# A hybrid attention and state-space layer: five places of local kernels on SyncE and three on ScalarE, feature stores held for two weight blocks, and the rest of u loaded in three parts

## The reference, cut to what matters

```python
h = rmsnorm(x, norm_mix_pre)
z = h @ w_in
q, k, v, u, gates = jnp.split(z, splits, axis=-1)
y_attn = windowed_gqa_sink(q, k, v, attn_sink) @ w_branch_attn
y_ssm = s5_bidirectional(u, ...) @ w_branch_ssm
g = jax.nn.sigmoid(gates.reshape(bsz, seq, N_BRANCH, D_MODEL))
merged = g[:, :, 0] * y_attn + g[:, :, 1] * y_ssm
x = x + rmsnorm(merged @ w_out, norm_mix_post)
# then a feed-forward block: gelu(dwconv3(h2 W_gate)) * (h2 W_up), W_down, rmsnorm
```

## Time and profile before

| | us |
|---|---|
| time before, median of 3 (2640.09 to 2646.72) | 2644.09 |
| the profiled execution's own time | 2639.97 |
| its span | 2638.2 |
| TensorE busy in the span | 2532.5 |
| input projection, to TensorE's first attention matmul | 0 to 264.3 |
| attention, to the first matmul on u | to 463.2 |
| gates and states, to TensorE's last matmul on the states | to 896.9 |

### The profile page before, as it was taken

One profiled execution on the slowest core, in us unless ns is written; L12 is line 12 of the kernel. 1 busy time (PEld: TensorE's weight loads), 2 busy tenths in 40 slices (PEclk: granted clock), 3 DMA queues, 4 the chain that ended last, 5 costly groups with the idle time before them and its releaser, 6 DMA issues. The chain is left out here.

```text
span 2638.2 us, 34575 instructions
## 1 busy us (share of the span) xinstructions
PE 2532.5 (96%) x12222; PEld 2082.1 (79%) x12222; DVE 1655.7 (63%) x2255; ACT 968.8 (37%) x1754; POOL 1022.0 (39%) x1217
## 2 busy tenths in 40 slices
PE   7999898999999899999989999999999999999898
PEld 6877786788887688888868888877888887788786
DVE  5201765795970184544687767788766776675876
ACT  5221776512212350124453333343333334532432
POOL 2073564387830000012244354335344435443543
PEclk9999999999999899999999999999999999999999
DMA  6483878644446636464424222224222224455465
GB/s 215 137 273 111 179 179 232 212 144 148 156 172 163 176 127 236 175 164 151 153 88 151 74 90 86 72 66 132 87 90 81 79 75 144 166 196 203 152 208 183
DMA packets 317957, 390.98 MB, mean 148 GB/s; under 512 B 51936, under 2 KB 250080, under 8 KB 309472
## 3 DMA queue, kind: packets, MB, share of 16 engines
q1 hardware_dynamic: 270816, 309.66, 38.0%
q10 hardware_dynamic: 41184, 46.78, 5.3%
q0 software_dynamic: 5792, 32.38, 3.4%
HBM read 255.07 MB, written 133.69 MB: 147 GB/s over the span
## 5 line engine op out<-in xcount | busy, mean ns | idle before, releaser
L531 PE MATMUL tl_banks<-gu_b_hi,gu_a_hi 128*128 128x512 f32 x1848 | 727.3, 394 | 32.0 <-DVE gu_b_lo L1988 18.5
L533 PE MATMUL tl_banks<-gu_b_lo,gu_a_hi 128*128 128x512 f32 x1848 | 724.4, 392 | 0.0
L532 PE MATMUL tl_banks<-gu_b_hi,gu_a_lo 128*128 128x512 f32 x1848 | 723.9, 392 | 0.0
L531 PEld LDWEIGHTS tl_banks<-gu_b_hi,gu_a_hi 128*128 128x128 f32 x1848 | 350.0, 189 | 116.8 <-issue 31.5
L533 PEld LDWEIGHTS tl_banks<-gu_b_lo,gu_a_hi 128*128 128x128 f32 x1848 | 349.5, 189 | 73.1
L532 PEld LDWEIGHTS tl_banks<-gu_b_hi,gu_a_lo 128*128 128x128 f32 x1848 | 350.1, 189 | 71.9
L1982 DVE TENSOR_TENSOR gu_a_lo<-gu_raw,gu_a_hi 128x512 fp32r<-128x512 f32 (+1 forms) x340 | 296.8, 874 | 148.2 <-ACT gu_a_hi L1679 148.1
L1679 ACT ACTIVATE gu_a_hi<-gu_raw 128x512 fp32r<-128x512 f32 (+1 forms) x340 | 208.7, 616 | 347.1 <-PE tl_banks L533 297.5
L1354 POOL TENSOR_TENSOR gu_s_one<-gu_raw 128x512 f32<-128x512 f32 (+1 forms) x68 | 91.7, 1349 | 344.3 <-DVE gu_a_lo L1982 206.6
L1367 POOL TENSOR_TENSOR gu_raw<-gu_s_one,gu_raw 128x512 f32<-128x512 f32 (+1 forms) x68 | 97.8, 1439 | 166.7 <-DVE gu_a_lo L1982 166.3
L148 PE MATMUL pi_banks<-pi_feat_hi,pi_w_hi 128*128 128x512 f32 (+1 forms) x344 | 132.2, 384 | 10.1 <-DVE pi_feat_lo L333 6.1
(11 more groups left out here) (315 smaller groups left out, 5001.1 us busy)
## 6 DMA issues: line engine op xcount, KB each, us to landing
gu_raw<-in_w_ffn_gate SPq DMA_DIRECT2D x44, 512.0 KB, 3.6
gu_raw<-in_w_ffn_up SPq DMA_DIRECT2D x44, 512.0 KB, 3.5
gs_w_raw<-in_w_in SPq DMA_DIRECT2D x40, 512.0 KB, 4.4
br_rows<-gates POOLq DMA_DIRECT2D x16, 1024.0 KB, 7.2
gu_raw<-f SPq DMA_DIRECT2D x32, 512.0 KB, 3.9
dn_y<-down_sums SPq DMA_DIRECT2D x16, 1024.0 KB, 4.9
down_sums<-dn_y SPq DMA_DIRECT2D x15, 1024.0 KB, 5.9
f<-gu_conv SPq DMA_DIRECT2D x11, 1025.0 KB, 5.1
```

The lines of the kernel that those rows point to most:

```text
L531: pe.matmul(out, w_hi, x_hi, start=first, stop=False, skip_group_check=again)
L532: pe.matmul(out, w_lo, x_hi, start=False, stop=False, skip_group_check=again)
L533: return pe.matmul(out, w_hi, x_lo, start=False, stop=last, skip_group_check=again)
```

## The change

The change has three parts. In the input projection SyncE waits for the last product of block 5 before it stores feature chunk 2, and for the last product of block 6 before chunk 3. At the end of attention SyncE issues five of the eight places of the local kernels and ScalarE, after its last copy, the other three; GpSimd issues none. In the last part of gates and states, u's rest comes in three parts (groups 17 to 20, 10 to 16, 0 to 9); partitions 0 to 63 still come by SyncE, partitions 64 to 127 by GpSimd, which waits for the last gate product; ScalarE loads none. Each half of a part has a semaphore of its own.

```diff
@@ stage_project_in, sync
             store_features(1)
             load_weights(8)
+            sync.wait_ge(product_done, number[5, CHUNKS - 1] + 1)
             store_features(2)
             load_weights(9)
+            sync.wait_ge(product_done, number[6, CHUNKS - 1] + 1)
             store_features(3)
@@ attention_and_tables
+    BY_SYNC = 5
         sync.wait_ge(kernels_ready, 1)
-        for l in range(SSM_L // 2):
+        for l in range(BY_SYNC):
             place_local(sync, l, local_placed)
@@ gpsimd
-        pool.wait_ge(kernels_ready, 1)
-        for l in range(SSM_L // 2, SSM_L):
-            place_local(pool, l, local_late)
@@ scalar
         copy_share(TILES - 1)
+        act.wait_ge(kernels_ready, 1)
+        for l in range(BY_SYNC, SSM_L):
+            place_local(act, l, local_late)
@@ gates_and_states
-    middle = first_mid // 2
+    u_starts = [first_mid - 4, first_mid - 11, 0]
-    u_parts = [slice(middle, first_mid), slice(0, middle)]
+    u_parts = [slice(first, last) for first, last in zip(u_starts, [first_mid] + u_starts)]
@@ gpsimd
         pool.dma_start(outof_flat[3], outof_scratch[3]).then_inc(last_table_in, 16)
+        pool.wait_ge(gate_done, N_PARTS)
+        load_groups(pool, u_rest, u_scratch, u_half_in, 1, u_parts)
@@ tensor, own_tokens
-                    pe.wait_ge(u_in[0 if g >= middle else 1], 2 * 16)
+                    part = sum(g < first for first in u_starts)
+                    pe.wait_ge(u_in[part], 16)
+                    pe.wait_ge(u_half_in[part], 16)
@@ scalar
-        load_groups(act, u_rest, u_scratch, u_in, 1, u_parts)
```

More of the change, by code:

```diff
@@ L3231, in _ @@
         copy_share(TILES - 1)
-    last = [(outof_stored, 4 * 16), (local_placed, SSM_L // 2 * 16), (local_late, SSM_L // 2 * 16)]
+        act.wait_ge(kernels_ready, 1)
+        for l in range(BY_SYNC, SSM_L):
+            place_local(act, l, local_late)
+    last = [(outof_stored, 4 * 16), (local_placed, BY_SYNC * 16), (local_late, (SSM_L - BY_SYNC) * 16)]
     return last + [(stored[s], TILES // 2 * N_KV * 16) for s in range(2)]
@@ L3314, in gates_and_states @@
     gate_stored = [m.pool_dma_sem("gate_stored0"), m.pool_dma_sem("gate_stored1")]
-    u_in = [m.sem("u_in0"), m.sem("u_in1")]
+    u_in = [m.sem(f"u_in{part}") for part in range(len(u_starts))]
+    u_half_in = [m.pool_dma_sem(f"u_half_in{part}") for part in range(len(u_starts))]
     y_done = m.sem("y_done")
```

## The result

The changed kernel takes 2632.15 us (median; 2629.0 to 2632.48) against 2645.71 us for the kernel before on the same chip: a ratio of 0.9949, 95% interval 0.9937 to 0.996, that is 13.5 us less (10.6 to 16.7). In a second comparison it took 2633.21 against 2646.72, ratio 0.9954 (0.9939 to 0.9968). The forecast was 2630.2, range 2624 to 2637.

What follows compares the result with a forecast made beforehand. TensorE was taken to bound the kernel, busy for 2532.5 of 2638.2 us. A 5.5, B 2.9 and C 5.5 sum to 13.9 us, off the median of 2644.09: 2630.2 us, range 2624 to 2637.

Steps and rivals of the forecast that it cites:

- A: Input projection: holding the feature stores removes TensorE's two waits for copies of u; wins 5.5 us, from 2.1 to 6.1.
- C: Late gates and states: three parts of u's rest remove TensorE's wait and slow restart; wins 5.5 us, from 3.0 to 6.9.
- The first wait: Input projection: block 4's u stores land at about 160, before 166.97, so TensorE's first wait for ScalarE's copy goes.
- the landing of block 5's stores: Input projection: block 5's u stores, due by 187.4, land at 186, between 178.4 and 189.3; the second wait goes.
- a wait for u's stores: Input projection: sign of a wrong prediction if such a wait turns up on TensorE; no size given.
- the second u wait stays: Input projection rival, chance 0.12: block 5's stores land at the far bound, 2.1 us won, time 2633.6 us.
- The stall: Input projection rival, chance 0.08: moves to block 7 as block 6's stores land at 212.7; 6.2 us lost, time 2635.7.
- B: Meeting after attention: without GpSimd's places its drain no longer holds TensorE; wins 2.9 us, from 1.5 to 3.6.
- the landing of the 2 MB: After the meeting: ScalarE and VectorE wait for it before first copies; a late one may take 1 us back.
- the 1.4 us given back for pair 4: Late gates and states: GELU of pair 4 waits for y's stores, slipping from 859.65 to about 861.5; up to 1.5 us.
- Halves in series: Loads of u's rest, rival, chance 0.17: SyncE's half served before GpSimd's; 2.2 us of wait stay, 3.7 won, time 2632.0.
- the last rival: Loads of u's rest, chance 0.04: GpSimd's parts take 12.7 us each, one after another; up to 9.6 us lost, time 2645.3.

Runs made afterwards that it cites:

- chunk 2 in halves: Changed kernel with feature chunk 2's high half stored one product earlier, low half where it was: 2627.97 us, ratio 0.9927; in a second comparison 2631.68 us, 0.9940.
- B alone: Kernel before with only the local kernels' places moved from GpSimd's queue to ScalarE's and SyncE's: 2641.43 us, ratio 0.9986.
- C with two parts: Kernel before with u's rest in two parts as before, second halves loaded by GpSimd instead of ScalarE's queue: ratio 0.9978.
- with whole parts: Kernel before with u's rest in three parts, each one transfer over 128 partitions, by SyncE alone: 2640.95 us, ratio 0.997.

## Why the prediction was right

**The sum.** 13.9 us were forecast on the median, and 13.5 measured. The terms were less good than their sum: A was 1.3 to 3.4 us too large, C 1.6 too small. That the sum is off by only 0.4 us is luck: the errors of A and C have opposite signs.

**A, 5.5 forecast, 4.2 and 2.1 measured.** The first wait went as worked out, with block 4's stores landing at 162.4 where about 160 was taken. The step that failed is the landing of block 5's stores: 186 was taken, from 5.77 MB at 370 GB/s, and 189.0 and 190.2 came, at the far bound of 189.3 and beyond it. So a wait for u's stores did turn up on TensorE, one of the signs that the prediction had named for being wrong. This is the rival "the second u wait stays", which had 0.12 and gave A 2.1 us; the second trace has just that. The trace of the changed kernel tells what the sum left out. DMA share in tenths and GB/s, 140 to 200 us in 40 slices of 1.5 us, then the queues in 172 to 180 and in 182 to 188:

```profile
DMA  9799999999955520003999999999855518999999
GB/s 112 213 397 408 411 410 407 415 345 280 244 192 186 187 78 0 0 0 139 365 380 353 306 338 346 351 307 285 171 116 184 182 39 317 378 382 388 388 326 342
```

```profile
q1 hardware_dynamic: 1093, 2.21, 84.1%
q10 hardware_dynamic: 461, 0.45, 18.0%
```

```profile
DMA packets 1327, 0.98 MB, mean 163 GB/s; under 512 B 46, under 2 KB 1271, under 8 KB 1327
q1 hardware_dynamic: 836, 0.50, 34.6%
q10 hardware_dynamic: 491, 0.48, 27.1%
```

From slice 28 on, 182 us, the rate is 116 to 184 GB/s for four slices, about 1 MB; the same shows in 156 to 161. About half of it is the end of SyncE's bytes (weights 9 stand last there), the other half is u's stores; nearly all packets are under 2 KB, and the engines are busy for only 62% of the time. At 370 GB/s this last megabyte would take 2.6 us, and it took 6.0: by this estimate some 3.4 us more, which leads from 186 to 189.4. Why the end is slow is open. Taking 2 MB out of the way of the stores brought their landing forward by 5.7 us and the whole 6.14 us home, so the run with chunk 2 in halves shows that the bytes beside them were the cause of the second wait. The 2.1 us between the two traces go with the slow clock, which the rival had counted as "up to 2.1". The stall did not move to block 7: no wait for a copy follows 192 us.

**B, 2.9 forecast, 3.0 measured at the meeting** (2.8 to 3.1 in five traces with 5 and 3). Each step of it is in the drains: SyncE's last, GpSimd's 0.70 us, TensorE 0.9 us behind it. But part of this gain can be lost again right behind the meeting, by TensorE's clock, which the prediction had not counted. The first 8 us from the first matmul on u (columns as the earlier trace rows), in the kernel before and in the two traces of the changed kernel:

```profile
463.19:471.19 8.00, 8.00 (x29) 6.77 (x30) 4.95 (x14) 4.53 (x12) 0.00 (x0) 0.78 0.88 272
```

```profile
454.78:462.78 8.00, 8.00 (x26) 6.65 (x27) 4.24 (x12) 3.91 (x11) 0.00 (x0) 0.69 0.77 217
```

```profile
458.43:466.43 8.00, 8.00 (x30) 6.86 (x31) 5.21 (x14) 4.77 (x13) 0.00 (x0) 0.81 0.80 232
```

In all three TensorE comes out of the idle stretch at the lower level of its clock (1.2 GHz; 0.50 in the first 2 us) and is busy from then on. The granted clock of these rows is a mean over both levels, and TensorE runs 29, 26 and 30 matmuls in the 8 us. At matmul 2860 the lead from the end of attention is 2.4 us in the first trace and 3.2 in the second, 3.3 in B alone, and 1.8 and 2.0 with chunk 2 in halves; in the table the difference stands under "else". What was named as late next, the landing of the 2 MB, took nothing of it: TensorE did not wait for copies in these matmuls, not even with a fourth place on ScalarE.

**C, 5.5 forecast, 7.1 measured** in every kernel that has it. The wait and its slow restart went, as worked out (6.92), and the step to pair 3 was 2.80 us instead of 2.99. The mis-sized term is the 1.4 us given back for pair 4: it came 0.85 us late, inside the room that the prediction had named (861.5 against 859.65) and did not trust. "Halves in series", at 0.17, fell in its main point: TensorE waited for no part, and the queues' rows show both moving bytes at once. The order did hold for the two queues of the kernel before, but they were not issued at the same time, as the prediction objected, and no run removes that doubt; GpSimd's loads, issued together with SyncE's, were not served behind all of them. The rate under the rival was real, too: 249 GB/s with halves and 414 with whole transfers. The Trainium skill, SBUF — State Buffer, section "Can I just issue two DMAs to hit both halves?", says that two transfers on the two halves of the partitions serialize, and that only one transfer over all 128 partitions reaches all ports. On the rate the trace agrees, with those 414 against 249 GB/s at full DMA share; taken as an order it holds here for the loads by SyncE and ScalarE and not for those by SyncE and GpSimd. GpSimd's parts did not come one after the other, as the last rival had it: they took 5.2, 9.2 and 13.4 us, issued within 1.6 us.

**The scale.** Putting the sum on the median and not on the profiled execution was right, and needed: the first trace of the kernel before was 5.7 us under the median of the comparison (2645.71), and profile against profile the change wins 10.0 us, by the medians 13.5.

## What to carry to other kernels

Work out a wait's cost from two instruction starts around it and an undisturbed step, as was done for A and C: the full 6.1 and 7.1 us came back once the last late transfer was out of the way. When a transfer must land by a date, look whether the last bytes of such a group go at the stretch's mean rate; here the last megabyte went at less than half of it, which was about the difference between 186 and 189 us. Follow a gain past the wait that it removes: at the meeting up to 1 us of 3 was lost in the next matmuls. And compare single traces place by place: the sum of two traces' differences hid a quarter of the gain in a tail that the change doesn't touch.

## What was not expected of the hardware

One software transfer of GpSimd's (256 KB) was enough for a drain of 5.46 us, and four took 7.45 and 7.35; the drain ended 0.1 to 0.2 us behind the landing of the last of them. Drains of SyncE and ScalarE behind transfers just issued took 0.2 to 0.6 us and ended before those had landed: in the kernel before SyncE's ended at 458.7, and its last store landed at 462.4. In the loads of u's rest SyncE's and ScalarE's queues moved their bytes one behind the other, GpSimd's and SyncE's side by side; in the input projection SyncE's and ScalarE's moved side by side too (2.21 and 0.45 MB in 172 to 180), so this is no rule for the queues. And the granted clock's fall near 193 us is not tied to the code alone: it is in both traces of the kernel before (0.83 in 190 to 200) and in one of two of the changed kernel, while two kernels with the old projection and the old waits were granted 1.00 there (C with two parts, and with whole parts) and passed it 1.9 and 2.0 us sooner.
